# Four modulation units moved from layer 1's attention to layer 2's, shift logits by VectorE's sums, prompt's projection units first in layer 2

## The chip, the cores and the metric

The kernel runs on one core of one Trainium2 chip. The metric is the time on the device in microseconds (us), lower is better. All data are fp32.

## The reference, cut

Two token groups, 128 prompt tokens and 128 sample tokens of width 1024, pass through two layers. Each layer is an attention and a mixture of 16 experts, each with pre-norm, shift, scale and a gated residual. Shift, scale and gate come from six slices of one linear of SiLU(c).

```python
m = jax.nn.silu(cond) @ w_mod[l] + b_mod[l]          # 6 x 1024: shift, scale, gate (attention); shift, scale, gate (experts)
sh, sc, g, shf, scf, gf = jnp.split(m, 6, axis=-1)    # for the prompt's cond and for the sample's
hp, hs = rmsnorm(xp) * (1 + sc_p) + sh_p, rmsnorm(xs) * (1 + sc_s) + sh_s
# layer 1: grouped-query attention and differential attention, layer 2: neighbourhood attention,
# the sample's queries see the sample's keys and 128 cached context keys
xp, xs = xp + g_p * op, xs + g_s * os_
# experts: softmax router, best group of 4, its top 2 experts
h = rmsnorm(x) * (1 + scf) + shf
scores = softmax(h @ w_router)
x = x + gf * sum_e gate_e * ((silu(h @ w_gate[e]) * (h @ w_up[e])) @ w_down[e])
```

The kernel also returns the new keys and values of the prompt. The weights of both layers, some 490 MB, are read from DRAM once.

## The kernel before, in words

**Loads.** SyncE issues all loads of weights, in the order in which its program is written, into a ring of six slots of 2 MB each, of which one unit fills one (`load`, L552 and L554). It waits before each for the unit that had the slot before (`room_for`, `read_at`: a modulation unit signals `mod_used`, another unit signals with its last product). A layer has these dense units: `("in", l, u)`, 512 columns of the input projection, `("out", l, u)`, 512 columns of the output projection, and `("mod", l, group, k)`, a quarter k of the rows of 2048 columns of the modulation's weights. Group 0 is shift and scale of the attention, group 1 the gate of the attention and the shift of the experts, group 2 scale and gate of the experts. `dense_units(l)` gives the order of the dense loads, with the last ones of layer 1 being those of groups of layer 2. `released(l)` gives the order in which their slots come free.

**Experts.** The 16 experts are run in 8 pairs of 12 units. Before a layer's experts begin, some of the first pairs' units are loaded early: `load_ahead`, `load_kept` (quarters of a unit, into buffers that the attention leaves), and `load_first(k)`, into the ring's slots as the attention releases them. In layer 1 all `load_first` stand behind the others (`free = 2 * l` is 0), in layer 2 the first two, the experts' first gate units, are issued ahead of them. Behind these each load waits for the product that used its slot: `load_early` for the rest of pairs 0 to 2, then a loop. The first gate products of the experts are line 1162.

**Order on TensorE and the others.** The attention is cut in 8 turns, four of the sample, then four of the prompt. In a turn scores (L973) are made two turns ahead, ScalarE makes the exponents from them (L1426), VectorE maxima (L1730), reciprocal and shares (L1739, L1750), TensorE transposes the shares (L857), ScalarE copies them (L1437, L1380), TensorE multiplies by the values (L1005, L1011, L1019). What TensorE does beside it stands in a table, `FILL[l]`: items at "front", "head", "keys", "scores" (ahead of the turns), at `(j,)` (in turn j, between transposes and values) and at j (behind the values). In an item's name the second number is the unit and the third the token group (1 sample, 0 prompt). The items: `("in", u, t)` is a projection unit, 8 products of 512 columns (L925); `("mod", l, group, k)` 8 products with `cond` (`mod`, L881) into `sums_bank`; `("modT", g)` and `("nextT", g)` the transposes of a finished group's sums (`mod_transposed`, L892), of this layer or the next; `("wo", u, t)` the output projection (L935); `("rc",)` the shift logits; `hT`, `hk`, `rt`, `xT`, `pos` norm, router and positions of the experts' tokens. VectorE walks the same table (`meanwhile`). On VectorE `mod` copies and adds up a group's result (`modc`, `gates`), and `out_project` (L1782, L1784) multiplies an output by the gate, held in `gbuf`, and adds it to x.

**Gates.** GpSimd writes the attention gates of a layer to DRAM (`spread_gates`, L787), and reads them back to all partitions (L793), into `gbuf`. In layer 2 it waits with the second until VectorE has added the expert outputs and TensorE is done with the sample's scores. `gates_taken` counts the groups whose gates VectorE has put away; SyncE waits for it before its last `load_kept`, too.

**Shift logits.** The router's product is made of normed rows without shift. What the shift adds is a row of 16 numbers, shift times `w_router`, which `shift_logits(l)` makes by 8 products of 128 x 16 (L1051). Layer 1's stands at `("rc",)`, turn 7. Layer 2's stands between the last two scatters of layer 1's experts, in `sums_bank`, and the copy to `rc` of VectorE signals `shift_taken`.

**Modulation of layer 2 in layer 1.** Groups 0 and 1 of layer 2 are read in layer 1: group 0 in turns 2 and 3 with its transposes in turn 4, group 1 at the turns 6 and 7 with its transposes at the end.

## Time and profile before

| | us |
|---|---|
| median of 3 runs | 1247.43 |
| the runs | 1246.78, 1247.43, 1249.86 |
| the profiled execution | 1245.62 |
| its span | 1243.7 |
| first product of layer 1's experts | 194.27 |
| first projection of layer 2 | 641.00 |
| first product of layer 2's experts | 803.78 |

The span is the time from the first to the last instruction in the trace of the profiled execution, whose own time on the device is 1.9 us longer. TensorE is busy for 1163.5 us of the span (94%), VectorE for 279.9, ScalarE for 187.3, GpSimd for 56.4. The granted clock is 0.989 of full speed over the span. The 494.15 MB of the DMA engines are moved at 397 GB/s in the mean, 420 to 431 GB/s while experts run and 182 to 335 GB/s in layer 2's attention. A time in the text is in us from the span's start. The profile counts two instructions for each product, so that a projection unit or a modulation unit, 8 products each, is x16.

### The profile page before, as it was taken

How to read it: one execution, taken by the hardware profiler on the slowest of the kernel's cores; microseconds unless marked ns; L12 is line 12 of the kernel's file. 1: busy time of each engine (PE TensorE's matmuls, PEld its weight loads, DVE VectorE, ACT ScalarE, POOL GpSimd, SP SyncE). 2: the span in 40 equal slices, each digit the busy share in tenths (PEclk: the TensorE clock that was granted, in tenths of full speed). 3: DMA queues.
4: the chain of work that ended last, by engine and by line, in shares of the span. 5: the costliest groups of instructions: out<-in, count | busy, mean ns of one | idle time of the engine just before them, and what ended most of it. 6: DMA issues, size and time to landing. Idle time of an engine off the chain costs nothing.

```text
span 1243.7 us, 13724 instructions
## 1 busy us (share of the span) xinstructions
PE 1163.5 (94%) x5507; PEld 509.5 (41%) x5507; DVE 279.9 (23%) x675; ACT 187.3 (15%) x439; POOL 56.4 (5%) x68
## 2 busy tenths in 40 slices
PE   4999999999988889989999999999999988989898
PEld 2445454443423233434344454653434423343433
DVE  1146533121010101021232354312021110102013
ACT  1224322010000000001021343210000100000010
POOL 0412000000000000000013020000000000000000
PEclk9999999999999999999999999999999999999999
DMA  9999999999999999999995578999999999999997
GB/s 376 386 373 380 414 420 429 421 431 428 428 427 428 428 428 429 429 427 428 418 392 182 196 262 335 391 374 418 428 428 428 427 427 428 428 429 428 428 423 310
DMA packets 63397, 494.15 MB, mean 397 GB/s; under 512 B 5859, under 2 KB 7027, under 8 KB 32117
## 3 DMA queue, kind: packets, MB, share of 16 engines
q1 hardware_dynamic: 60304, 485.85, 94.3%
q0 software_dynamic: 2864, 7.46, 1.9%
q8 instruction: 33, 0.54, 0.2%
q10 hardware_dynamic: 180, 0.17, 0.0%
q14 instruction: 16, 0.12, 0.0%
HBM read 490.69 MB, written 3.16 MB: 397 GB/s over the span
## 4 chain that ended last, share of the span: by engine, by line
PE 71%; DMA 22%; issue 4%; ACT 1%; SPq 1%; DVE 1%; POOL 0%; DVEq 0%; POOLq 0%
PE bank L1162 40%; PE bank L925 12%; DMA ring<-in_w_up 7%; DMA ring<-in_w_gate 7%; DMA ring<-in_w_down 6%; PE bank L935 3%; PE bank L1117 3%; PE bank L1126 3%; PE bank L881 3%; DMA ring<-in_w_in_ab 2%; PE bank L857 2%; PE bank L1188 1%; PE bank L973 1%; PE bank L1218 1%; PE bank L1019 0%
## 5 line engine op out<-in xcount | busy, mean ns | idle before, releaser
L1162 PE MATMUL bank<-ring,hT 128*64 128x512 f32 x2520 | 572.7, 604 | 50.6 <-issue 19.3
L1162 PEld LDWEIGHTS bank<-ring,hT 128*64 128x64 f32 x2520 | 191.2, 139 | 402.6 <-issue 393.6
L925 PE MATMUL bank<-ring,hT 128*128 128x512 f32 x320 | 141.9, 601 | 3.1 <-DMA ring<-in_w_in_ab 2.4
L925 PEld LDWEIGHTS bank<-ring,hT 128*128 128x128 f32 x320 | 60.4, 192 | 80.0 <-issue 77.4
L1940 DVE TENSOR_TENSOR work<-work,bank 128x512 f32<-128x512 f32 x56 | 38.5, 688 | 165.1 <-PE bank L1126 164.9
L1933 DVE TENSOR_TENSOR work<-work,bank 128x512 f32<-128x512 f32 x32 | 22.0, 688 | 222.0 <-PE bank L1162 197.9
L1162 PE MATMUL bank<-work,hT 128*64 128x512 f32 x284 | 69.6, 593 | 0.0
L1117 PE MATMUL bank<-work 128*128 128x128 f32 x512 | 60.4, 276 | 0.0
L1117 PEld LDWEIGHTS bank<-work 128*128 128x128 f32 x512 | 58.7, 192 | 1.7 <-issue 1.6
L1485 ACT ACTIVATE hT<-bank 128x512 f32<-128x512 f32 x32 | 19.0, 595 | 255.3 <-PE bank L1218 255.3
L935 PE MATMUL bank<-ring,work 128*128 128x512 f32 x128 | 56.5, 594 | 0.3 <-DVE work L1759 0.3
L1981 DVE COPY work<-bank 128x512 f32<-128x512 f32 x14 | 9.7, 692 | 207.1 <-PE bank L1162 207.1
L1126 PE MATMUL bank<-work 128*128 128x512 f32 x112 | 51.8, 605 | 0.0
L881 PE MATMUL bank<-ring,cond 128*32 128x512 f32 x384 | 47.0, 614 | 2.1 <-DMA ring<-in_w_mod 1.7
L1188 PE MATMUL bank<-ring,hT 128*64 128x512 f32 x192 | 42.9, 595 | 3.9 <-DMA ring<-in_w_down 3.9
L1921 DVE TENSOR_TENSOR work<-work,bank 128x512 f32<-128x512 f32 x32 | 22.0, 688 | 106.9 <-ACT work L1494 106.9
L1162 PEld LDWEIGHTS bank<-work,hT 128*64 128x64 f32 x284 | 22.7, 137 | 42.1 <-issue 40.7
L1512 ACT ACTIVATE work<-bank 128x512 f32<-128x512 f32 x14 | 8.4, 597 | 191.0 <-PE bank L1162 191.0
L1494 ACT ACTIVATE work<-bank 128x512 f32<-128x512 f32 x32 | 19.1, 597 | 108.5 <-PE bank L1162 108.5
L935 PEld LDWEIGHTS bank<-ring,work 128*128 128x128 f32 x128 | 23.7, 190 | 27.6 <-issue 27.6
L1126 PEld LDWEIGHTS bank<-work 128*128 128x128 f32 x112 | 20.1, 189 | 31.4 <-issue 31.4
L1656 DVE TENSOR_REDUCE hss<-bank 128x8 f32<-128x512 f32 (+1 forms) x16 | 10.5, 658 | 90.2 <-ACT bank L1385 90.2
(214 smaller groups left out, 731.2 us busy)
## 6 DMA issues: line engine op xcount, KB each, us to landing
ring<-in_w_gate SPq DMA_DIRECT2D x56, 2048.0 KB, 17.6
ring<-in_w_up SPq DMA_DIRECT2D x50, 2048.0 KB, 17.2
ring<-in_w_down SPq DMA_DIRECT2D x46, 2048.0 KB, 17.2
ring<-in_w_mod SPq DMA_DIRECT2D x23, 2048.0 KB, 11.8
work<-in_w_up SPq DMA_DIRECT2D x8, 2048.0 KB, 16.1
ring<-in_w_down SPq DMA_DIRECT2D x14, 1024.0 KB, 14.6
ring<-in_w_in_c SPq DMA_DIRECT2D x6, 2048.0 KB, 21.2
ring<-in_w_in_ab SPq DMA_DIRECT2D x4, 2048.0 KB, 21.5
```

Source lines behind the costliest of these rows:

```text
L857: ins = pe.transpose(b[:, i * P:(i + 1) * P], src, K("ident"))
L881: ins = pe.matmul(out, cond[:, 2 * k + r, :], cols, start=(k, r) == (0, 0), stop=(k, r) == (3, 1), tile_position=(0, 32 * j))
L925: ins = pe.matmul(b[:, 0:n], hT[:, c, t * P:(t + 1) * P], w[:, c, 0:n], start=i == 0, stop=i == DC - 1)
L935: ins = pe.matmul(b[:, :], oT(l, t, c), w[:, c, :], start=c == 0, stop=c == DC - 1)
L1117: ins = pe.matmul(bank[2 if first and h else h][:, c * P:(c + 1) * P], htok(t)[:, at:at + P], pick[:, t, :], start=t == 0, stop=t == 1)
L1126: pe.matmul(bank[4 + 2 * t + h][:, :], GT[:, t, :], yd[:, h * UC:(h + 1) * UC], start=True, stop=True).then_inc(m["scattered"], 1)
L1162: ins = pe.matmul(bank[banks[j]][64 * e:64 * e + 64, :], lhs[:, 4 * h + c, 64 * e:64 * e + 64], weights(e, c, j), start=(h, c) == (0, 0), ...
L1188: ins = pe.matmul(bank[banks[j]][64 * e:64 * e + 64, :], lhs[:, 4 * h + c, 64 * e:64 * e + 64], rows4[slots[e]][:, c, j * UC:(j + 1) * UC] ...
L1494: act.activation(sg[:, h * UC:(h + 1) * UC], bank[h][:, :], ACT.Sigmoid).then_inc(m["sig_done"], 1)
L1921: dve.tensor_tensor(hid[:, half], sg[:, half], bank[h][:, :], ALU.mult).then_inc(m["gate_taken"], 1)
L1933: dve.tensor_tensor(hid[:, half], hid[:, half], bank[2 + h][:, :], ALU.mult).then_inc(m["hid_done"], 1)
L1940: dve.tensor_tensor(y[:, t, cols], y[:, t, cols], bank[4 + 2 * t + h][:, :], ALU.add).then_inc(m["y_added"], 1)
```

## The change

1. The four units of `("mod", 1, 1, k)` are no longer loaded and used in layer 1. They are loaded in layer 2 behind its projection units and used at "scores" and in turn 0 there, their transposes stand in turn 1.
2. Layer 1's places: one unit of `("mod", 1, 0, k)` in each of turns 2 and 3, the other two in turn 7, where those of group 1 stood; `("nextT", 0)` stands at the end. SyncE loads two of these units ahead of the output projection's, two behind.
3. In layer 2 the prompt's projection units 0 to 3 stand at "head" and "keys", and the sample's units 4 and 5 (its values) at "scores", between modulation units.
4. `shift_logits`: VectorE multiplies `w_router` by the shift (128 x 128 numbers) and sums over the 8 chunks (`shares_of_shift`, 128 x 16), and one product with the table of ones sums over partitions. It stands in turn 1 of layer 1 and turn 2 of layer 2; the product behind layer 1's experts and its semaphores are gone.
5. In layer 2 SyncE issues three `load_first` ahead of the others in place of two, in layer 1 two in place of none (`free`), and its waits for `gates_taken` and a group's transposes follow the new order.

```diff
     0: {"front": [("in", 0, 1), ("hT", 0, 0), ("in", 1, 1), ("in", 2, 1), ("in", 3, 1)],
...
-        2: [("modT", 2), ("mod", 1, 0, 0), ("mod", 1, 0, 1)],
+        2: [("modT", 2), ("mod", 1, 0, 0)],
...
     if l == 0:
-        return mods(0, 0) + inputs + mods(0, 1) + mods(0, 2) + mods(1, 0) + out + mods(1, 1)
+        later = mods(1, 0)
+        return mods(0, 0) + inputs + mods(0, 1) + mods(0, 2) + later[0:2] + out + later[2:4]
     scales = mods(1, 2)
-    return inputs + scales[0:2] + out + scales[2:4]
+    return inputs + mods(1, 1) + scales[0:2] + out + scales[2:4]
...
-                free = 2 * l
+                free = 2 + l
...
-                sp.wait_ge(gates_taken, 3 + l)
-                sp.wait_ge(filled, fill(("modT", 1, 1 + l)))
+                sp.wait_ge(gates_taken, 2 + 2 * l)
+                sp.wait_ge(filled, fill(("modT", 1, 2 * l)))
...
             def shift_logits(l):
 
-                pe.wait_ge(*emptied_by(("modT", l, 1)))
-                pe.wait_ge(ld_router, 32)
-                b = bank_free(("rc", 0)) if l == 0 else sums_bank
-                for c in range(DC):
-                    ins = pe.matmul(b[:, 0:NE], modc[:, l, 2, 0, c:c + 1].to_broadcast([P, P]), wr[:, c, :], start=c == 0, stop=c == DC - 1)
-                ins.then_inc(filled if l == 0 else shift_ready, 1)
+                pe.wait_ge(ld_const, 16)
+                pe.wait_ge(shift_summed, l + 1)
+                b = bank_free(("rc", l))
+                pe.matmul(b[:, 0:NE], K("ones"), shares_of_shift[:, :], start=True, stop=True).then_inc(filled, 1)
...
-                        if (l, t) == (0, 1):
-                            shift_logits(1)
...
                 modulate(l, 1, 0)
                 if l == 0:
-                    mod(1, 1)
+                    mod(1, 0)
...
+                if group == 1:
+                    dve.wait_ge(*emptied_by(name))
+                    dve.wait_ge(ld_router, 32)
+                    part = cmp[:, 0:128].rearrange("p (c e) -> p c e", c=DC)
+                    then(dve.tensor_tensor(part, wr[:, :, :], modc[:, l, 2, 0, :].unsqueeze(2).to_broadcast([P, DC, NE]), ALU.mult))
+                    dve.tensor_reduce(shares_of_shift[:, :], part.rearrange("p c e -> p e c"), AX.X, ALU.add).then_inc(shift_summed, 1)
...
-                if l == 0:
-                    name = ("rc", 0)
-                    dve.wait_ge(filled, fill(name))
-                    dve.tensor_copy(rc[:, :], bank_of(name)[:, 0:NE]).then_inc(emptied["dve"], 1)
...
+                    elif item[0] == "rc":
+                        name = ("rc", l)
+                        dve.wait_ge(filled, fill(name))
+                        dve.tensor_copy(rc[:, :], bank_of(name)[:, 0:NE]).then_inc(emptied["dve"], 1)
```

What stands in a row on the engines, in the order of their programs, follows for three places. Line numbers of the changed kernel are 2 or 3 lower than those of the kernel before.

TensorE in layer 1 from the end of turn 1 to turn 3, before: x8 of L881 are one modulation unit, L857 transposes, L973 scores, L1011 values, L892 the transposes of a modulation group.

```order
L892 MATMUL bank<-const,m 128x128 x4
L881 MATMUL bank<-ring,cond 32x512 x16
L857 MATMUL bank<-const,work 128x128 x8
L973 MATMUL bank<-work 128x128 x4
L1011 MATMUL bank<-work 64x256 x4
L881 MATMUL bank<-ring,cond 32x512 x8
L857 MATMUL bank<-const,work 128x128 x4
L881 MATMUL bank<-ring,cond 32x512 x8
L857 MATMUL bank<-const,work 128x128 x2
```

The same place, of the changed kernel:

```order
L890 MATMUL bank<-const,m 128x128 x4
L879 MATMUL bank<-ring,cond 32x512 x8
L857 MATMUL bank<-const,work 128x128 x8
L971 MATMUL bank<-work 128x128 x4
L1009 MATMUL bank<-work 64x256 x4
L879 MATMUL bank<-ring,cond 32x512 x8
L857 MATMUL bank<-const,work 128x128 x6
```

Each of the two turns has one modulation unit in place of two.

TensorE in layer 2 from the transposes of the sample's queries and keys to turn 0, before: L925 products are projection units (x8 is one), L1019 values.

```order
L857 MATMUL bank<-const,work 128x128 x24
L925 MATMUL bank<-ring,hT 128x512 x16
L973 MATMUL bank<-work 128x256 x8
L925 MATMUL bank<-ring,hT 128x512 x16
L857 MATMUL bank<-const,work 128x128 x8
L973 MATMUL bank<-work 128x256 x4
L1019 MATMUL bank<-work 64x128 x8
L925 MATMUL bank<-ring,hT 128x512 x8
```

The same place, of the changed kernel:

```order
L857 MATMUL bank<-const,work 128x128 x24
L923 MATMUL bank<-ring,hT 128x512 x16
L971 MATMUL bank<-work 128x256 x8
L879 MATMUL bank<-ring,cond 32x512 x8
L923 MATMUL bank<-ring,hT 128x512 x8
L879 MATMUL bank<-ring,cond 32x512 x8
L923 MATMUL bank<-ring,hT 128x512 x8
L857 MATMUL bank<-const,work 128x128 x8
L971 MATMUL bank<-work 128x256 x4
L1017 MATMUL bank<-work 64x128 x8
L879 MATMUL bank<-ring,cond 32x512 x8
L923 MATMUL bank<-ring,hT 128x512 x8
L879 MATMUL bank<-ring,cond 32x512 x8
```

At "scores" four modulation and projection units stand in turn (each x8), where two projection units stood, and turn 0 has two modulation units more. The projection units of the sample's values stand behind those of the prompt.

SyncE at the end of layer 1's dense loads and the start of the experts' early loads, before: L552 is a modulation unit, L554 an output unit, L564 a unit of an expert.

```order
L552 DMA ring<-in_w_mod 128x2x2048 [waits bank_filled]
L552 DMA ring<-in_w_mod 128x2x2048 [waits mod_used]
L554 DMA ring<-in_w_out_ab 128x8x512 [waits mod_used] x2
L552 DMA ring<-in_w_mod 128x2x2048 [waits mod_used] x4
L564 DMA work<-in_w_up 128x4096 [waits bank_filled]
```

The same place, of the changed kernel:

```order
L554 DMA ring<-in_w_out_ab 128x8x512 [waits bank_filled]
L554 DMA ring<-in_w_out_ab 128x8x512 [waits mod_used]
L552 DMA ring<-in_w_mod 128x2x2048 [waits mod_used] x2
L564 DMA ring<-in_w_gate 128x4096 [waits mod_used] x2
L564 DMA work<-in_w_up 128x4096 [waits bank_filled]
```

The last two of the four modulation units behind the output projection are gone. The experts' first two gate units stand there, ahead of the first `load_ahead`.

## Rows read from the trace of the kernel before

**Rows 1.** windows: us, busy time of PE, PEld, DVE, ACT, POOL, clock, share, GB/s

```profile
200.00:400.00 200.00, 190.76 (x938) 79.42 (x936) 29.36 (x64) 18.99 (x33) 0.00 (x0) 1.00 1.01 427
...
675.00:690.00 15.00, 15.00 (x54) 8.08 (x53) 8.14 (x6) 3.04 (x6) 2.31 (x1) 1.00 0.00 0
803.00:808.00 5.00, 4.22 (x20) 1.61 (x20) 0.00 (x0) 0.60 (x1) 0.00 (x0) 1.00 0.69 268
640.00:800.00 160.00, 157.43 (x697) 84.31 (x696) 62.97 (x164) 52.02 (x143) 22.69 (x20) 1.00 0.76 281
```

**Rows 2.** chain of waits, pairs 1 and 2: start us, us, what

```profile
254.26 20.75 PE bank L1162 x96
...
304.35 20.75 PE bank L1162 x96
```

**Rows 3.** page, part 6: a modulation unit: KB, us to landing

```profile
ring<-in_w_mod SPq DMA_DIRECT2D x23, 2048.0 KB, 11.8
```

**Rows 4.** timeline of SyncE's issues, layer 1, then layer 2

```profile
194.22 0.33 SPq L647 DMA_DIRECT2D m<-in_w_down  x1
201.35 0.80 SPq L564 DMA_DIRECT2D ring<-in_w_down  x2
211.20 0.81 SPq L564 DMA_DIRECT2D ring<-in_w_gate  x2
...
745.10 0.55 SPq L635 DMA_DIRECT2D ring<-in_w_down  x1
759.66 0.33 SPq L564 DMA_DIRECT2D work<-in_w_up  x1
```

**Rows 5.** line views: the issue of 194.22, then those of 201.35

```profile
DMA to landing us min/median/max: 15.1/15.1/15.1
...
DMA to landing us min/median/max: 12.8/15.1/17.4
```

**Rows 6.** line view: a modulation unit issued at 692.83 into an idle queue

```profile
DMA to landing us min/median/max: 7.1/7.1/7.1
```

**Rows 7.** chain of waits, layer 1: start us, us, what

```profile
145.59 0.47 PE bank L892 x4
...
154.87 1.85 PE bank L881 x16
...
178.19 1.69 PE bank L1051 x16
...
194.27 7.09 PE bank L1162 x32
```

**Rows 8.** timeline, layer 1: start us, us, engine, line, what, idle before

```profile
128.74 0.29 DVE L1599 TENSOR_TENSOR cmp<-wr,modc 128x128 f32<-128x128 f32 x1
...
154.90 0.60 ACT L1437 ACTIVATE work<-bank 128x512 f32<-128x512 f32 x1 [4.01 <-PE bank L857]
...
179.02 0.69 DVE L1784 TENSOR_TENSOR x<-x,tmp 128x512 f32<-128x512 f32 x1
```

**Rows 9.** chain of waits, then timeline, layer 2

```profile
641.00 7.11 PE bank L925 x16
...
718.02 1.09 PE L1019 MATMUL bank<-work 128*64 128x128 f32 x16 [0.56 <-ACT work L1437]
```

**Rows 10.** L793 in layer 2, then in layer 1; L787 in layer 2

```profile
DMA to landing us min/median/max: 4.4/4.8/5.1
...
DMA to landing us min/median/max: 8.7/10.3/11.9
...
DMA to landing us min/median/max: 12.2/12.6/13.1
```

**Rows 11.** timeline, layer 2, turns 5 and 6

```profile
762.46 0.88 DVE L1750 TENSOR_SCALAR work<-work,rinv 128x128 f32<-128x128 f32 x4
...
767.29 0.60 PE L857 MATMUL bank<-const,work 128*128 128x128 f32 x4
```

More of the change, by code:

```diff
@@ L113 @@
         0: [("in", 4, 0), ("modT", 1)],
-        1: [("T", 0), ("mod", 0, 2, 2), ("mod", 0, 2, 3)],
-        2: [("modT", 2), ("mod", 1, 0, 0), ("mod", 1, 0, 1)],
-        3: [("mod", 1, 0, 2), ("oT", 1), ("mod", 1, 0, 3)],
-        4: [("wo", 0, 1), ("nextT", 0)],
+        1: [("T", 0), ("rc",), ("mod", 0, 2, 2), ("mod", 0, 2, 3)],
+        2: [("modT", 2), ("mod", 1, 0, 0)],
[2 rows of a table added]
         5: [("wo", 1, 1)],
-        (6,): [("mod", 1, 1, 0)],
         6: [("oT", 0)],
-        (7,): [("mod", 1, 1, 1)],
[2 rows of a table removed]
[2 rows of a table added]
     1: {"front": [("in", 0, 1), ("hT", 0, 0), ("in", 1, 1), ("in", 2, 1), ("in", 3, 1)],
[5 rows of a table removed]
-        2: [("mod", 1, 2, 1)],
[2 rows of a table added]
+        "scores": [("mod", 1, 1, 0), ("in", 4, 1), ("mod", 1, 1, 1), ("in", 5, 1)],
+        0: [("mod", 1, 1, 2), ("in", 4, 0), ("mod", 1, 1, 3)],
+        1: [("T", 0), ("modT", 1), ("mod", 1, 2, 0), ("in", 5, 0)],
+        2: [("rc",), ("mod", 1, 2, 1)],
         3: [("mod", 1, 2, 2)],
@@ L286, in build @@
         rc = sb("rc", [P, NE])
+        shares_of_shift = sb("shares_of_shift", [P, NE])
         lg = sb("lg", [P, NE])
@@ L400, in build @@
         half_squares = sem("half_squares")
-        shift_ready, shift_taken = sem("shift_logits_ready"), sem("shift_logits_taken")
+        shift_summed = sem("shift_summed")
         chunk_ready = {"act": sem("chunk_modulated_act"), "dve": sem("chunk_modulated_dve")}
@@ L865, in mod @@
                     pe.wait_ge(mod_emptied, 3 * l + group)
-                if (l, group, k) == (1, 2, 0):
-                    pe.wait_ge(shift_taken, 1)
                 for r in range(2):
@@ L1219, in hidden_transposed @@
                     ins.then_inc(m["ht_done"], 1)
-                last = number["modT", 1, 1] if l == 0 else number["count", 1]
+                last = number["modT", 1, 0] if l == 0 else number["count", 1]
                 before, behind = ([jobs[k][0] for k in range(last - 6, last + 1) if (bank_of(jobs[k][0]) is bank[1]) == first] for first in (True, False))
@@ L1642, in largest_logit @@
                 if t == 0:
-                    dve.wait_ge(*(emptied_by(("rc", 0)) if l == 0 else (shift_taken, 1)))
+                    dve.wait_ge(*emptied_by(("rc", l)))
                     dve.scalar_tensor_tensor(out=lg[:, :], in0=bank_of(name)[:, 0:NE], scalar=ss[:, 0:1], in1=rc[:, :],
@@ L1990, in experts @@
                 if l == 0:
-                    mod(1, 1)
+                    mod(1, 0)
                 pair(0)
@@ L2009, in experts @@
                     add_last(end, 0, 1)
-                    dve.wait_ge(shift_ready, 1)
-                    dve.tensor_copy(rc[:, :], sums_bank[:, 0:NE]).then_inc(shift_taken, 1)
                     norm_asked(1, 0, 0)
```

13 rows, old and new, of the table FILL are left out of this document.

## The prediction

> **What bounds the kernel now.** Read the table by stretches first. In 200 to 400 us the 16 DMA engines are busy all the time (share 1.01) at 427 GB/s; from 675 to 690 us their share is 0.00 while TensorE is busy 15.00 of 15.00 us; over 640 to 800 us TensorE is busy 157.43 of 160 us, at 281 GB/s [rows 1]. So there are two regimes. While the experts of a layer run, a pair of experts needs 12 units of 2048 KB [rows 3], 25.17 MB, which at 427 GB/s is 58.9 us. The chain of waits shows the same piece in pair 1 (254.26) and in pair 2 (304.35), so TensorE does a pair in 50.1 us [rows 2]. TensorE starts with a store of early loads and uses it up; after that the stream of loads sets the time. In layer 2's attention it is the other way round: TensorE sets the time and the DMA idles. The end of each layer's experts is therefore "when the stream last ran dry, plus bytes over rate", and it runs dry where SyncE has no free buffer to load into.
>
> **Part 1, the loads leave layer 1.** Four units of 2048 KB [rows 3] are 8.39 MB, at 427 GB/s 19.6 us. Layer 1's experts would end 19.6 us earlier if the stream never ran dry. It does. SyncE's last load before the experts' first product is issued at 194.22 [rows 4] and lands 15.1 us later [rows 5], at 209.3. The next, at 201.35, waits until that product gives a buffer back. So at 201.35 there are 209.3 - 201.35 = 7.9 us of work queued. If TensorE reaches the experts X earlier, and 19.6 us of loads are gone, the queue is dry for 19.6 - X - 7.9 us. X can't be over 4 x 1.85 + 0.47 + 1.69 = 9.6 us, all TensorE work that goes (below), so it is dry in any case, and the gain of the stream is not 19.6 but X + 7.9, less what starting a dry queue costs. A load into an empty queue landed 7.1 us after its issue [rows 6]; 2048 KB at 427 GB/s take 4.9; so 2.2 us. At the next issue (211.20, where the second load of 201.35 still had to land, 201.7 + 17.4 = 219.1 [rows 4, 5]) 7.9 us of work become 7.9 - 5.7 = 2.2, just that latency; I take 0.3 us off. Gain of layer 1: X + 5.4.
>
> **X, TensorE's gain in layer 1**, along the chain [rows 7]:
> - Turns 2 and 3 lose a unit each: 3.7 us. But VectorE now makes the shift sums in turn 1, a product of 128 columns (0.29 [rows 8]) and a sum over as many, 0.6 to 0.7 us ahead of its maxima of the next turn, and TensorE's values of turn 2 wait for ScalarE's copy behind those: 0.7 us back. The one-column product, and the values of turn 4, which now meet ScalarE's copy, take 0.5. Left 2.5.
> - The transposes of a modulation group (0.47 at 145.59) go to the end of the attention, where those of the next group stood: 0.4. Sum 2.9.
> - The units of turns 6 and 7 stood where TensorE waits for ScalarE's copy. The unit goes from 154.87 to 156.72, the copy from 154.90 to 155.5 [rows 7, 8], and the values need the copy: of 1.85 us 1.1 is gained, the rest becomes a wait. In turn 7 the transposes need VectorE's shares, made behind the output addition of turn 5, which is itself only 4 us earlier: 0.5 more. Sum 4.5.
> - The eight products of the shift logits (178.19, 1.69, so to 179.88) go, but the transposes behind them need VectorE's addition to x, which ends at 179.02 + 0.69 = 179.71 [rows 7, 8]. Gain 0; the wait takes their place.
>
> So X = 4.5, between 2.9 (nothing in turns 6 and 7) and 9.6 (all of it). Layer 1's experts end 4.5 + 5.4 = **9.9 us** earlier; bounds 8.3 and 15.0. They stay bound by the stream: TensorE has 58.9 - 50.1 = 8.8 us a pair in hand.
>
> The second set of shift products, between the last two scatters of layer 1, stands beside VectorE's and GpSimd's norm of the sample rows, which the next projection needs and they don't: 0 us.
>
> **Part 2, the units come into layer 2.** TensorE is busy there, so they are paid. A unit costs 1.85 us [rows 7], four 7.4. The transposes of the group take 0.5 to 0.7; the one-column product and VectorE's copy, 0.2. The first values of layer 2 waited 0.56 us for ScalarE [rows 9], which had a prompt unit's squares to make first; now value units stand there, which it doesn't touch: -0.5. The loads cost nothing: the first goes out when the layer's fifth projection unit is done, on the old clock at 641.0 + 5 x 7.11 = 676.6 [rows 9], lands 7.1 us later in an idle stretch [rows 1, 6], and is used three units, 21 us, after its issue. The value units of the sample rows come late, but only the first values need them.
>
> One wait grows: that for the gates. GpSimd writes them to DRAM and spreads them back after the last prompt unit, as now. Before, that spreading took 4.4 to 5.1 us with SyncE's queue nearly empty (no issue from 745.10 to 759.66); the same two transfers took 8.7 to 11.9 in layer 1 beside a full queue [rows 4, 10]. Now two more units are queued at that time: the last one of group 2, which waits for the last prompt unit, and the experts' third gate unit, brought forward. So I take 8.7, the first half lands 4.3 us later. VectorE's output addition waits for it, then come shares and maxima. The shares ended at 762.46 + 0.88 = 763.34 and TensorE asked for them at 767.29, 3.95 us later [rows 11]. Of 4.3 us 0.35 come through there, and about 1 more through the last turn's exponents on ScalarE: 1.3 us.
>
> Sum for the start of layer 2's experts: 7.4 + 0.7 + 0.2 - 0.5 + 1.3 = **+9.1 us**. Bounds: 5.7 (the gates not later, and all idle of the stretch, 160 - 157.4 = 2.6, filled) and 14.7 (the gates as in C below). The experts of layer 2 then run as before, only later: in 803 to 808 us the DMA share is 0.69 [rows 1], all early loads had landed when they began, so a third gate load that lands sooner is worth nothing, and the stream starts anew with TensorE.
>
> **Sum.** 9.1 - 9.9 = -0.8 us. Against the profile's own time: span 1243.7 to 1242.9, run 1245.62 to 1244.8. The median of the runs, 1247.43, lies 1.8 us above the profiled run; forecast 1246.6, no change that can be told (about 0.3%, 3.7 us, is what a measurement can tell).
>
> **Two rules of the Trainium skill.** The page "DMA: Bandwidth & Descriptors", section "Queues, rings and completion order", says that each DMA engine takes turns between the queues that have work for it, packet by packet. By it the gates' transfers share with SyncE's units and don't stand behind them, which speaks for 8.7 and against C; layer 1's 8.7 to 11.9 us agree. Its section "Where 436 GB/s comes from" gives about 358 GB/s as the limit of one core's reads from memory; four units would then be 23.4 us. The trace has 427 GB/s, and the measurement decides.
>
> **Rivals.**
> - **A, all of TensorE's gain comes through.** X = 9.6. For: some waits are chains that start at an output projection that is itself earlier. Against: copy and addition end late whatever TensorE does [rows 8]. Then 9.1 - 15.0 = -5.9: 1241.5. Chance 0.16.
> - **B, the stream doesn't run dry.** 9.1 - 19.6 = -10.5: 1236.9. For: no load of layer 1's experts finds the queue empty now. Against: the sum of part 1, dry for any X below 11.7. Chance 0.06.
> - **C, slower: the gates come late.** If their write and spreading stand behind the two added units, 2 x 4.9 = 9.8 us, TensorE waits 9.8 - 3.95 = 5.9 us and the 1 behind it: 6.9 in place of 1.3, so -0.8 + 5.6 = +4.8: 1252.2. It costs from the point where the first half lands 3.95 us later than now, and makes over 0.3% from 8.7 us. For: the write of 4 KB took 12.2 to 13.1 us there already [rows 10]. Against: layer 1's rows. Chance 0.21.
> - That the change doesn't do what it says is excluded by the order of instructions: the units are gone from one place and stand in the other.
>
> **How the numbers follow.** Forecast 0.55, A 0.16, B 0.06, C 0.21; 0.02 for a slower cause that I don't see. The forecast's own terms spread it by about 3.5 us each way, which puts 0.03 of it beyond 3.7 us on the fast side; on the slow side C is that tail. Faster by over 0.3%: 0.16 + 0.06 + 0.03 = 0.25. Slower: 0.21 + 0.02 = 0.23. Within: 0.52. The range takes in A and C and leaves out B and the tails, 1241.0 to 1252.3.
>
> **What the profile after would show.** Right: DMA share well below 1 for 5 to 8 us between 191 and 199 us; the first expert product at about 189.8 instead of 194.27 [rows 7]; layer 2's first projection at about 631 instead of 641.0 [rows 9]; from there to layer 2's first expert product 9.1 us more than before; idle before the transposes of x where the shift products stood. Wrong: expert start in layer 1 near 185 (A); DMA share 1.0 from 100 to 600 us and layer 2's first projection at 621 (B); VectorE waiting 15 us or more for the spread gates, with TensorE idle before the transposes of turn 6 (C).

## The result, and the profile after

The changed kernel runs at **1253.28 us** (median of 6, 1252.37 to 1256.86) against 1247.11 us (median of 6) of the kernel before: ratio 1.0059, 95% interval 1.0048 to 1.0071. Slower by 6.2 us, by more than 0.3%. The forecast was no change, 1246.6 us with a range up to 1252.3. The profiled execution took 1252.37 us against 1245.62.

The page of the changed kernel, the span and two lines of part 2 (40 equal slices of 31.3 us: the DMA engines' busy tenths, and GB/s):

```profile
span 1250.6 us, 13674 instructions
...
DMA  9998979999999999999997789899999999999997
GB/s 375 393 371 347 385 292 377 425 430 427 428 427 427 428 428 429 431 427 428 417 385 242 269 315 396 333 368 412 422 427 428 427 429 429 429 428 429 428 422 297
```

The DMA line of the kernel before reads 9 up to the 21st slice; here the fourth (94 to 125 us) reads 8 and the sixth (156 to 188 us) 7, with 292 GB/s.

The chain of waits of the changed kernel (start us, us, what): the first product of layer 1's experts, one in the stretch in which TensorE waits for loads, layer 2's first projection, and the first product of layer 2's experts.

```profile
193.82 7.09 PE bank L1158 x32
...
362.37 7.09 PE bank L1158 x32
...
637.48 7.10 PE bank L923 x16
...
809.32 7.09 PE bank L1158 x32
```

The rows of the kernel before that answer to the second and the last (the first and the third are in [rows 7, 9]):

```profile
367.23 7.09 PE bank L1162 x32
...
803.78 7.26 PE bank L1162 x32
```

So the time went like this:

| stretch | forecast | measured |
|---|---|---|
| first expert product of layer 1 (194.27 before) | 4.5 earlier | 0.45 earlier |
| what the stream of loads gives beyond that, at the product of 367.23 us before (now 362.37, 4.86 earlier) | 5.4 | 4.4 |
| the same, at layer 2's first projection (641.00 to 637.48, 3.52 earlier) | 5.4 | 3.1 |
| from there to layer 2's first expert product (162.78 to 171.84) | 9.1 longer | 9.06 longer |
| the rest of the span (439.9 to 441.3) | 0 | 1.4 longer |
| span | 0.8 shorter | 6.9 longer |

The rows overlap: the second and the third tell of the same gain at two places, and the span is -3.5 + 9.1 + 1.4. Layer 2's attention came out as forecast. Layer 1 gave 3.5 in place of 9.9 us. Where the first line went is in turn 1 of layer 1. The windows of the changed kernel (columns as in [rows 1]):

```profile
120.00:130.00 10.00, 7.58 (x53) 3.23 (x55) 5.93 (x17) 4.17 (x12) 3.21 (x5) 0.83 0.50 186
...
170.00:180.00 10.00, 8.42 (x30) 4.25 (x29) 1.71 (x4) 2.63 (x8) 0.00 (x0) 1.00 0.53 216
200.00:205.00 5.00, 4.44 (x31) 2.65 (x28) 1.63 (x8) 2.05 (x3) 0.00 (x0) 1.00 0.73 233
```

The same windows of the kernel before:

```profile
120.00:130.00 10.00, 9.81 (x87) 4.28 (x80) 8.39 (x27) 5.72 (x21) 2.61 (x4) 1.00 0.93 338
...
170.00:180.00 10.00, 10.00 (x46) 6.17 (x46) 2.03 (x6) 2.20 (x7) 0.00 (x0) 1.00 1.04 433
200.00:205.00 5.00, 4.44 (x31) 2.65 (x29) 1.41 (x8) 1.61 (x3) 0.00 (x0) 1.00 0.98 402
```

From 120 to 130 us TensorE is busy 7.58 us in place of 9.81, its granted clock is 0.83, and the DMA share is 0.50. The timeline of TensorE there, then the chain's piece behind it (two modulation units), then SyncE's next issue:

```profile
122.24 0.36 PE L1048 MATMUL bank<-shares_of_shift,const 128*128 128x16 f32 x2 [3.40 <-ACT work L1420]
```

```profile
122.60 5.31 PE bank L879 x32
```

```profile
125.52 2.78 SPq L552 DMA_DIRECT2D ring<-in_w_mod  x2
```

The one-column shift product (L1048) waits 3.40 us, and what releases it is ScalarE's exponents (L1420), not VectorE's sums. It writes into a PSUM bank, and the banks go round seven places in the order in which the program asks for them (`bank_free` waits for the one that had the bank seven places before). Seven places before stand the first scores of turn 3, which TensorE has just made, and ScalarE reads them only after VectorE's maxima. VectorE's sums themselves had been ready since 118.3 us. The two modulation units, which need no new bank and so covered that time before the change, stand behind the product. After the idle 3.40 us the clock falls: the two units take 5.31 us, where the kernel before took 3.61 for the same two. They also give up their ring slots late: SyncE's next load goes out at 125.52; before, the corresponding one went out at 120.92. In the kernel before, the two units in the chain, and SyncE's issue:

```profile
119.00 3.61 PE bank L881 x32
```

```profile
120.92 2.08 SPq L554 DMA_DIRECT2D ring<-in_w_out_ab  x2
```

The windows show a second thing, which isn't the product's doing. From 170 to 180 us the DMA share is 0.53 in place of 1.04. SyncE's issues around it, changed and before:

```profile
168.31 0.33 SPq L564 DMA_DIRECT2D ring<-in_w_gate  x1
177.79 0.80 SPq L647 DMA_DIRECT2D work<-in_w_down  x2
```

```profile
162.61 6.46 SPq L564 DMA_DIRECT2D ring<-in_w_gate  x3
...
178.22 0.80 SPq L647 DMA_DIRECT2D work<-in_w_down  x2
```

The issue near 178 us comes at nearly the same time in both. Before it, the kernel before had three units of 2048 KB to queue; the changed kernel had issued two of these at 133 us already and had one left, and the queue ran empty (share 0.19 from 175 to 180 us). So the stream runs dry twice, there and at 195 to 205 us (0.88, then 0.73). The forecast had one dry stretch, 191 to 199 us; from 190 to 195 us the share is 1.01.

### The profile page after: what moved, and what is told of

Read it like the earlier page. It is cut to its first block, busy times and chain, and to the rows that moved or that the text cites. A ratio compares the mean times of both kernels' runs of the same rounds, so it can differ in the third digit from the quotient of the medians.

```text
span 1250.6 us, 13674 instructions
## 1 busy us (share of the span) xinstructions
PE 1163.3 (93%) x5479; PEld 507.0 (41%) x5479; DVE 281.1 (22%) x679; ACT 187.3 (15%) x439; POOL 56.3 (5%) x68
## 4 chain that ended last, share of the span: by engine, by line
PE 67%; DMA 25%; issue 4%; DVE 2%; ACT 1%; SPq 1%; POOL 0%; DVEq 0%; POOLq 0%
PE bank L1158 38%; PE bank L923 12%; DMA ring<-in_w_up 10%; DMA ring<-in_w_down 8%; DMA ring<-in_w_gate 5%; PE bank L933 3%; PE bank L1113 3%; PE bank L879 3%; PE bank L1122 2%; DMA ring<-in_w_in_ab 2%; PE bank L857 1%; PE bank L1184 1%; PE bank L1212 1%; PE bank L971 1%; ACT work L1431 0%
## 5 line engine op out<-in xcount | busy, mean ns | idle before, releaser
L1420 ACT ACTIVATE work<-bank,nm 128x256 f32<-128x256 f32 (+1 forms) x64 | 26.0, 420 | 27.5 <-DVE nm L1728 27.5
```

Source lines behind the costliest of these rows:

```text
L1420: ins = act.activation(PR[:, j % 2, h, 0:nk], bank_of(("S", l, t, b, e))[:, i * nk:(i + 1) * nk], ACT.Exp, bias=nm[:, j % 2, h:h + 1], sca ...
```

## Experiments

The theory after this comparison, **M**: the shift product waits for its bank; TensorE's loss in layer 1 is this wait, with what the clock and the held ring slots add. Against it stood **V**: VectorE's two added operations are late themselves, and hold up scores and exponents wherever the product stands; and **S**: the term for the stream was wrong, that is, loads are worth their bytes or nothing. All ratios are to runs of the kernel before beside them, on the same chip (their medians: 1246.27 us beside runs 1 to 4, 1246.74 beside 5 to 8, 1246.54 beside 9 to 12). They are the ratios on record; the quotient of two medians can differ from them, by 0.0014 at most (run 11).

| run | first expert product | layer 2's first projection | first expert product of layer 2 | median us | ratio (95%) |
|---|---|---|---|---|---|
| before | 194.27 | 641.00 | 803.78 | 1247.11 | |
| changed | 193.82 | 637.48 | 809.32 | 1253.28 | 1.0059 (1.0048 to 1.0071) |
| 1, product behind the units | 189.60 | 633.61 | 805.53 | 1249.73 | 1.0029 (1.0018 to 1.0039) |
| 2, before + shift sums | 202.03 | 647.58 | 810.98 | 1253.88 | 1.0050 (1.0036 to 1.0064) |
| 3, before, 4 loads cut | 195.47 | 639.29 | 802.07 | 1245.02 | 0.9988 (0.9980 to 0.9997) |
| 4, before, 1 load cut | 194.20 | 639.50 | 802.28 | 1244.33 | 0.9984 (0.9975 to 0.9992) |
| 5, as 2, product behind | 194.79 | 639.85 | 803.17 | 1247.80 | 1.0002 (0.9991 to 1.0012) |
| 6, before + layer 2's order | 195.67 | 641.40 | 803.55 | 1246.36 | 0.9993 (0.9984 to 1.0002) |
| 7, changed, 8 products in layer 1 | 188.81 | 632.57 | 804.61 | 1247.64 | 1.0005 (0.9996 to 1.0014) |
| 8, as 7, unit in turn 6 for turn 3 | 189.64 | 632.86 | 803.59 | 1246.45 | 1.0000 (0.9991 to 1.0008) |
| 9, as 7, unit in turn 6 for turn 7 | 188.72 | 632.83 | 803.55 | 1246.27 | 0.9993 (0.9982 to 1.0003) |
| 10, as 7, unit in turn 3 for turn 7 | 191.28 | 634.70 | 805.41 | 1248.35 | 1.0009 (0.9998 to 1.0019) |
| 11, changed, again | 195.00 | 639.36 | 811.24 | 1255.64 | 1.0059 (1.0042 to 1.0076) |
| 12, before, again | 194.65 | 640.82 | 803.59 | 1246.75 | 0.9996 (0.9985 to 1.0007) |

**Run 1: the changed kernel with the shift product behind the two units.**

```diff
-        1: [("T", 0), ("rc",), ("mod", 0, 2, 2), ("mod", 0, 2, 3)],
+        1: [("T", 0), ("mod", 0, 2, 2), ("mod", 0, 2, 3), ("rc",)],
```

> The changed kernel with one item moved: in layer 1's turn 1 the one-column shift product stands behind the two modulation units, not ahead of them. Theory M (the product waits for its PSUM bank, which still holds scores that ScalarE has not read, and the two units that could cover this stand behind it): the 3.6 us wait at 118.6 to 122.2 goes, with it the clock of 0.83 in 120 to 130 us; the first expert product is at 189.5 instead of 193.82, and since the stream of loads hangs on TensorE from 201 us on, the end moves with it: 1249.0 instead of 1253.3. Rival V (VectorE's two added operations are late themselves, wherever the product stands): first expert product at 193 or later, time 1253.

Its window of 120 to 130 us, the first expert product and one in the loads' stretch, from the chain:

```profile
120.00:130.00 10.00, 9.39 (x82) 4.73 (x74) 8.50 (x25) 6.23 (x23) 2.09 (x3) 1.00 0.92 356
```

```profile
189.60 7.09 PE bank L1158 x32
...
359.07 7.09 PE bank L1158 x32
```

The wait is gone, the clock is 1.00, the DMA share 0.92. The first expert product is 4.2 us earlier than in the changed kernel, layer 2's first projection 3.9, the median 3.6 us. M holds; V doesn't explain the loss (what is left of it is in run 5). TensorE now gains 4.67 us in layer 1, where 4.5 were forecast. The stream is still dry at 170 to 175 us (share 0.15), so that hole is the missing loads' and not the wait's.

**Run 2: the kernel before with VectorE's shift sums and the one-column product in place of the eight products, and nothing else**, product at the head of turn 1 of layer 1 and of turn 2 of layer 2 (the edit, cut: the old products and their semaphores go as in the change).

```diff
-        1: [("T", 0), ("mod", 0, 2, 2), ("mod", 0, 2, 3)],
+        1: [("T", 0), ("rc",), ("mod", 0, 2, 2), ("mod", 0, 2, 3)],
...
-        2: [("mod", 1, 2, 1)],
+        2: [("rc",), ("mod", 1, 2, 1)],
...
+                pe.wait_ge(shift_summed, l + 1)
+                b = bank_free(("rc", l))
+                pe.matmul(b[:, 0:NE], K("ones"), shares_of_shift[:, :], start=True, stop=True).then_inc(filled, 1)
```

> The kernel before with the shift logits by VectorE's sums and nothing else changed (product at the head of layer 1's turn 1 and of layer 2's turn 2; all four units stay in layer 1). Theory (the wait is a loss of TensorE only, and costs at the end only where the stream of loads hangs on TensorE): first expert product of layer 1 3.5 to 5 us later than 194.27, near 198.5, but 7.9 us of loads are still queued there, so layer 2's first projection stays at 641 within 1 us; time 1247.5, same as before. Rival (the shift logits cost the whole loss of the change, in any surroundings): 1252 to 1253.

Its window of 120 to 130 us, the product's wait, SyncE's next issue:

```profile
120.00:130.00 10.00, 6.59 (x38) 1.90 (x35) 7.08 (x19) 3.96 (x14) 4.25 (x7) 0.66 0.27 89
```

```profile
123.74 0.58 PE L1049 MATMUL bank<-shares_of_shift,const 128*128 128x16 f32 x2 [3.41 <-ACT work L1421]
```

```profile
127.95 2.81 SPq L555 DMA_DIRECT2D ring<-in_w_out_ab  x2
```

I was wrong here: I expected the queue to take up the loss. The same wait, 3.41 us, a clock of 0.66, and the two output units, issued at 120.92 before, go out at 127.95, 7.0 us later, with a DMA share of 0.27. (This trace was 1.3 us behind that of the kernel before already ahead of the wait, see run 5.) In this kernel all units are in layer 1 and the stream isn't dry later (no window of 5 us from 130 to 225 us has a share under 0.97), and so a hole in it counts in full: from 110 to 135 us the DMA engines moved 2.6 MB less than before, 6.1 us at 427 GB/s, and layer 2's first projection is 6.6 us later. The 7.9 us that are queued at 201 us cover a late TensorE, but not a late issue at 121 us. The shift logits, which I had priced at 1.2 us in layer 1 (0.7 for the sums, 0.5 for the product and the values of turn 4), cost nearly as much by themselves as the whole change: 1.0050 against 1.0059.

**Runs 3 and 4: the kernel before with four, or one, of the group's loads cut to an eighth.** TensorE's work stays; part of the modulation is left out.

```diff
+                    if (l, group) == (1, 1) and k in (0, 1, 2, 3):
+                        sp.dma_start(rows2[slot][:, :, 0:256], src[:, :, 0:256]).then_inc(dense_ld[slot], 16)
+                    else:
+                        sp.dma_start(rows2[slot][:, :, :], src).then_inc(dense_ld[slot], 16)
```

> The kernel before with its four loads of modulation group 1 of layer 2 cut to an eighth (256 of 2048 columns, so these units use what was in the buffer before: part of the modulation is left out); TensorE's work is the same. 17.2 us of loads at 427 GB/s are gone, X is 0. Theory (the stream runs dry at 201 us, where 7.9 us of work are queued): gain at layer 2's first projection 4.3 to 5.4 us (636), time 1242. Rival (the stream doesn't run dry, loads are worth their bytes): gain 17, projection at 624, time 1230.

> The kernel before with one of these four loads cut to an eighth (part of the modulation left out), 4.3 us of loads less. Theory (7.9 us are queued at 201 us, so a first unit is worth its bytes and the later ones next to nothing): gain 4.3 us, projection at 636.7, time 1243, within 1 us of the kernel with four cut. Rival (gain in proportion to bytes, a quarter of what four give): 1 to 1.4 us, time 1246.

The product in the loads' stretch, with four cut, then with one cut and that kernel's last products of layer 1 (chain of waits; 367.23 and 626.86 before):

```profile
364.38 7.09 PE bank L1165 x32
```

```profile
362.87 7.09 PE bank L1165 x32
```

```profile
623.65 8.78 PE bank L1191 x32
```

One cut load gives 4.36 us there, its full bytes (4.3). Four give 2.85, with a first expert product that is 1.2 us later, so 4.05 beyond TensorE. S falls in both readings: the first unit counts in full, the other three count nothing, since from 201 us on the stream hangs on TensorE. But I missed the other place: at layer 2's first projection the gain is 1.71 us with four cut and 1.50 with one, not 4.3 and more, and the medians are 1.3 and 1.9 us below before, not 4. In the kernel with one cut all of what is missing has a row. The last load that the end of layer 1 waits for is issued 4.31 us earlier than before (605.43 to 609.74), but takes 18.09 us to land in place of 16.99, and the last products of layer 1 take 8.78 us in place of 7.09 (granted clock 0.69 from 625 to 630 us, 1.00 before). That load and those products in the kernel before:

```profile
609.74 16.99 DMA ring<-in_w_down
...
626.86 7.09 PE bank L1188 x32
```

**Run 5: run 2 with the product behind the units.**

> The kernel before with the shift logits by VectorE's sums, as in the run that had them ahead of the two modulation units of layer 1's turn 1, but now with the product behind these units. Theory M (the product waits for a PSUM bank that holds scores not yet read; the units behind it are held, they free ring slots late, and the stream of loads, which sets the end of layer 1 when all units are in it, stands still): no idle DMA between 121 and 130 us beyond what the kernel before has, first expert product at 194.3 to 195.3, layer 2's first projection at 641 to 642, time within 1 us of before. Rival V (VectorE's added sums hold up scores and exponents wherever the product stands): first expert product at 198 or later, time 1251 or more.

```profile
120.00:130.00 10.00, 9.40 (x86) 4.27 (x78) 8.43 (x27) 5.53 (x20) 2.55 (x4) 1.00 0.95 332
```

The first expert product is at 194.79, the ratio 1.0002: the loss of run 2 is gone by the place of one instruction. (Projection 639.85, a little earlier than expected.)

VectorE's sums do cost TensorE something, and it shows once a spread of the traces is taken out. The traces differ by up to 1.6 us already at 114 us, ahead of anything that the change touches on TensorE in layer 1. The transposes of a modulation group there, before and in run 5:

```profile
114.36 0.63 PE L892 MATMUL bank<-const,m 128*128 128x128 f32 x4
```

```profile
114.12 0.63 PE L891 MATMUL bank<-const,m 128*128 128x128 f32 x4
```

From these transposes to the first expert product it is 79.90 to 79.91 us in all five traces whose layer 1 is that of the kernel before on TensorE (before, runs 3, 4, 6, 12), and 80.67 us in run 5. So V was right for 0.8 us, where the prediction had 0.7 for the sums; the rest of the loss of run 2 was the place of the product. In this kernel the 0.8 us don't reach the end, which hangs on the loads.

**Run 6: the kernel before with layer 2's order of projection units alone.**

```diff
-        "head": [("in", 4, 1), ("in", 5, 1)],
-        "keys": [("in", 0, 0), ("in", 1, 0)],
-        "scores": [("in", 2, 0), ("in", 3, 0)],
+        "head": [("in", 0, 0), ("in", 1, 0)],
+        "keys": [("in", 2, 0), ("in", 3, 0)],
+        "scores": [("in", 4, 1), ("in", 5, 1)],
```

> The kernel before with only the order of layer 2's projection units changed (the prompt's units 0 to 3 at head and keys, the sample's units 4 and 5 at scores). The prediction's term: the wait of 0.56 us of the first values for ScalarE goes and nothing takes its place, so from layer 2's first projection to its first expert product 162.3 instead of 162.78 us, time 0.5 us lower than before, which is not to be told from no change. Rival (the value units now come so late that the first turn's values or VectorE's scores wait for them): 163.5 or more.

From projection to expert product 162.15 us, 0.63 less: as forecast (0.5), too small to be told in the median. It shows another thing: its first expert product is 1.4 us later than before with the same layer 1, and layer 2's first projection only 0.4. That is how a layer bound by its loads takes a late TensorE. The 1.4 us stand there at 114 us already (transposes at 115.77 in place of 114.36): the first expert product scatters by that much with one and the same program.

**Run 7: the changed kernel with layer 1's shift logits by the eight products in turn 7.**

```diff
-        1: [("T", 0), ("rc",), ("mod", 0, 2, 2), ("mod", 0, 2, 3)],
+        1: [("T", 0), ("mod", 0, 2, 2), ("mod", 0, 2, 3)],
...
-        7: [("hT", 1, 1), ("wo", 0, 0), ("rt", 1), ("hk", 1), ("wo", 1, 0), ("xT",), ("mod", 1, 0, 2),
+        7: [("hT", 1, 1), ("wo", 0, 0), ("rt", 1), ("hk", 1), ("wo", 1, 0), ("rc",), ("xT",), ("mod", 1, 0, 2),
```

> The changed kernel with layer 1's shift logits as in the kernel before: eight products in turn 7, no sums on VectorE in layer 1; layer 2 as changed. Theory M: TensorE's wait of 3.4 us in turn 1 is gone, and with it VectorE's 0.65 us and the one-column product: first expert product at 188.5 to 189.5 (the eight products hide behind VectorE's addition to x), the end follows it: 1248.5 to 1249.5 instead of 1253.3. Rival (the eight products are paid, 1.7 us): first expert product at 190.5 or later.

```profile
188.81 7.09 PE bank L1166 x32
...
357.25 7.09 PE bank L1166 x32
```

The first expert product is at 188.81, so the eight products hide behind VectorE's addition to x, as the prediction had it. The ratio is 1.0005 (median 1247.64, below the 1248.5 to 1249.5 expected): undoing the shift logits of layer 1 gives back nearly all that the change lost. Counted from the transposes at 114 us, the first expert product comes 74.16 us later here, 74.95 in run 1: the 0.8 us of VectorE's sums again.

**Runs 8, 9 and 10: places for the units.** All have the eight products in layer 1 and, in layer 2, the moved group's transposes behind the next modulation unit.

```diff
-        1: [("T", 0), ("modT", 1), ("mod", 1, 2, 0), ("in", 5, 0)],
+        1: [("T", 0), ("mod", 1, 2, 0), ("modT", 1), ("in", 5, 0)],
```

SyncE's order of loads follows where a unit changes its place. Run 8 moves `("mod", 1, 0, 1)` from turn 3 to `(6,)`, run 9 `("mod", 1, 0, 2)` from turn 7 to `(6,)`, run 10 the same unit from turn 7 to turn 3.

> A version made from what the runs showed: layer 1's shift logits by eight products in turn 7, one of layer 2's group 0 units moved from turn 3 into turn 6 of layer 1, where TensorE waits for ScalarE's copy and it costs about 0.75 of its 1.85 us, and in layer 2 the transposes of the moved group behind the next modulation unit (0.67 us of waiting). Theory (from 201 us on the stream hangs on TensorE, so what TensorE gains the end gains): first expert product at 187.5 to 188.5, layer 2's first projection at 631, its first expert product 171.2 us later, time 1246.5, equal to the kernel before within 1 us. Rival (the stream is bound by its own dry places ahead of 190 us, where ring slots are held): first expert product earlier but the first projection of layer 2 no earlier than 633.5, time 1249.

> The changed kernel with layer 1's shift logits by eight products (as in the run of that name), the moved group's transposes of layer 2 behind the next modulation unit, and one of the two units of turn 7 of layer 1 in turn 6. From the two runs before: in turn 6 such a unit costs 0.7 us (outputs at 157.21 instead of 156.40), in turn 7 it is on TensorE's path with 1.85. Theory: first expert product at 187.7 (188.81 less 1.1), layer 2's first projection at 631.5, then 170.7 us to its first expert product, time 1245, 1.5 us below the kernel before. Rival (turn 7's unit is hidden too, and turn 6's is paid): first expert product at 189.5.

> As the kernel with the unit in turn 6, but with this unit in turn 3 as a second one there. The run without any unit in turn 3 had the output projection at 135.51 against 135.41 with one: in turns 2 and 3 TensorE waits for VectorE's maxima. Theory (that wait has room for a second unit in part): output projection at 136 to 137, first expert product at 187.5 to 188.5. Rival (no room left): output projection at 137.3, first expert product at 188.8.

The start of the first output projection with one unit in turn 3 (run 7), none (run 8) and two (run 10), from the chain of waits:

```profile
135.41 6.87 PE bank L933 x16
```

```profile
135.51 6.87 PE bank L934 x16
```

```profile
137.30 6.87 PE bank L933 x16
```

Read as they stand, the one unit of turn 3 is free and the second is paid in full. But the three traces are not equally late at 114 us (transposes at 114.65, 115.39 and 114.73). Counted from there the projection starts after 20.76 us with one unit, 20.12 with none and 22.57 with two: the first unit costs 0.6 of its 1.85 us, the second 1.8. I missed run 8 for that reason: its unit gave up 0.6 us in turn 3 and cost 0.7 in turn 6, and the first expert product stayed where it was (74.25 us from the transposes, 74.16 in run 7). Run 9 missed too: moving the unit of turn 7 to turn 6 gave 0.2 us (73.93), not 1.1. Run 10's rival was nearer (projection as it said), but its first expert product came later still, at 191.28; why, no run shows. The transposes behind the unit took 1.3 us off layer 2: 170.73, 170.72 and 170.72 us in these three, 172.04 in run 7. The best of them, run 9, has 0.9993 (0.9982 to 1.0003): none beats the kernel before by more than the measurement tells.

**Runs 11 and 12: the two kernels once more.**

> The changed kernel once more, for a second trace. The layer 2's experts took 1.3 us longer after it than before it (437.92 to 436.59 us), with no difference in their loads. Theory (it is the spread of executions): in the second traces of the two kernels this difference is another, of either sign, within 1.5 us; what stands ahead of it repeats: 443.66 and 171.84 us. Rival (the change costs the experts of layer 2 a fixed amount): again 1.3.

> The kernel before once more, for a second trace beside that of the changed one on the same chip. Theory: 446.7 us from the first expert product to layer 2's first projection, 162.8 from there to its first expert product, and 436.6 to 438 us for the rest, since 436.59 is the lowest of eight traces. Rival: 436.6 again.

The product in the loads' stretch, changed and before:

```profile
365.48 7.09 PE bank L1158 x32
```

```profile
366.98 7.09 PE bank L1162 x32
```

The ratio repeats, 1.0059. In the second pair the span from the first expert product of layer 2 is 442.1 us changed and 440.7 before (the two expectations count to a point 3.3 us ahead of the span's end), again 1.4 longer, so my theory (spread alone) lost this pair. The stretches ahead of it in run 11 are 444.4 us (443.7 in the first trace) and 171.9 (171.8). Over all traces it is 440.8 to 442.4 (mean 441.7) in the seven with units in layer 2, and 439.9 to 442.2 (mean 440.9) in the seven without. The ranges overlap; whether the change costs layer 2's experts 0.8 to 1.4 us stays open, and no run was made that tells why.

## Why the prediction was wrong

**What bounds the kernel: right, but for a dry place.** Layer 1's experts are bound by a stream that is dry at 201 us once units are taken out (DMA share 0.73 from 200 to 205 us, 0.98 before), layer 2's attention by TensorE. The longer dry place, 165 to 180 us, was not foreseen, and the sign that the prediction named, a share well below 1 between 191 and 199 us, came late and in part: 1.01 from 190 to 195 us, 0.88 from 195 to 200.

**X, the failing step: "The one-column product, and the values of turn 4, which now meet ScalarE's copy, take 0.5."** The product was priced as an instruction, not as a place in the rotation of the banks; its wait for a bank was not in the sum at all. The sum was 2.9 us up to the output projections; the second of these, and the third, in the chain of waits of the changed kernel:

```profile
148.79 6.88 PE bank L933 x16
...
161.41 6.87 PE bank L933 x16
```

and before:

```profile
147.56 6.87 PE bank L935 x16
...
161.84 6.87 PE bank L935 x16
```

At the second projection TensorE is 1.2 us late in place of 2.9 early, 4.1 us off. The wait of 3.40, the product's 0.36 and the 1.70 that the two units lose by the clock (5.31 against 3.61) make 5.5 us, where the sum had 1.2 for all that the shift logits cost ahead of this projection: 4.3 us more than priced, less the 0.2 us by which this trace was ahead at 114 us. Run 1, with the product behind the units, brings X to 4.67. The rest of the step holds: turns 6 and 7 were to give 1.6 and give 1.7 (1.2 late to 0.4 early), and the eight products in turn 7 were hidden (run 7). In the changed kernel the transposes of x wait for VectorE where they stood:

```profile
179.33 0.94 PE L857 MATMUL bank<-const,x 128*128 128x128 f32 x6 [1.58 <-DVE x L1780]
```

**X + 5.4, mis-sized.** The form is right (runs 3 and 4). Against the first trace of before, the part beyond X at 362 us is 4.4 in the changed kernel and 2.5 in its second trace, 3.5 in run 1, 4.0 in run 3, 4.5 in run 7, 2.7 in run 9. At layer 2's first projection it is 3.1 and 2.4, 2.7, 2.9, 3.0, 2.6. I had taken off 2.2 us for one load into an empty queue, and 0.3 for the next issue. The landings of the two loads issued at 200.90 us, and of the two issued at 210.75:

```profile
DMA to landing us min/median/max: 7.7/9.9/12.2
...
DMA to landing us min/median/max: 9.1/11.3/13.6
```

The first pair's later load took 12.2 us in place of 17.4: 5.2 us beyond X, near the 7.9 - 2.2 of the sum. The second pair's took 13.6 in place of 17.3, 3.7 us beyond X: the next issue cost 1.5 us (2.2 in run 1, 1.1 in run 4), not 0.3. The loss between 362 us and the end of the layer has a row as well. The load that the layer's last products wait for:

```profile
604.89 18.31 DMA ring<-in_w_down
```

It is issued 4.85 us earlier than before (609.74), so until then nothing was lost, and takes 1.3 us longer to land (18.31 against 16.99); in run 1 it takes 0.9 us longer, in run 4 1.1. Why it takes longer stays open. With run 1's X the layer gives 7.4 us, not 9.9. So of the 7.7 us between the forecast span (0.8 shorter) and the measured one (6.9 longer) X has 4.1, the stream's term 2.3, and the open rest behind layer 2's attention 1.4.

**Layer 2, +9.1: right to 0.1 us, with terms that cancel.** I had 1.3 us for late gates. VectorE's wait, TensorE's asking for the shares behind it, and the landing of the two spreading transfers, changed kernel:

```profile
767.79 0.69 DVE L1778 TENSOR_TENSOR tmp<-bank,gbuf 128x512 f32<-128x512 f32 x1 [10.38 <-DMA gbuf<-gate_rows]
...
768.52 0.69 DVE L1780 TENSOR_TENSOR x<-x,tmp 128x512 f32<-128x512 f32 x1
...
769.33 0.87 DVE L1746 TENSOR_SCALAR work<-work,rinv 128x128 f32<-128x128 f32 x4
...
772.61 0.60 PE L857 MATMUL bank<-const,work 128*128 128x128 f32 x4
```

```profile
DMA to landing us min/median/max: 7.4/8.0/8.6
```

The first half took 7.4 us (I took 8.7), the addition ends at 768.52 + 0.69, and TensorE asks at 772.61, 2.4 us after the shares are made (769.33 + 0.87): no wait. The Trainium skill, page "DMA: Bandwidth & Descriptors", section "Queues, rings and completion order", has the engines take turns between queues; 7.4 to 8.6 us beside two queued units agree with it. In place of that term stands one that I had not: the transposes of the moved group wait for a bank too.

```profile
735.33 0.72 PE L890 MATMUL bank<-const,m 128*128 128x128 f32 x4 [0.67 <-ACT work L1420]
```

0.67 us. Four units 7.4, transposes 0.72, product 0.4, this wait 0.7, the order -0.6 (run 6) make 8.6; 0.5 us of the 9.06 has no row of its own. Two runs narrow it. Runs 2 and 5 have layer 2's shift logits without the four units and take 163.40 and 163.32 us for this stretch, 162.78 before: 0.5 to 0.6 us for the product with VectorE's sums, not 0.4. And the transposes' place cost 1.3 us (runs 8 to 10), twice the wait that has a row.

**The rivals.** A and B fell: X was below the forecast, and the stream ran dry. C's time (1252.2) is nearest to the result by luck, since its mechanism did not happen: TensorE waits for no gates. A slower outcome by a cause I did not see had 0.02 of my chances; it was what happened. **The range**, 1241.0 to 1252.3, missed the median by 1.0 us; the bank's wait was in none of its ends.

## What to carry to other kernels

A short instruction is as dear as the buffer it asks for: before moving one in a schedule with rotating banks, count back the rotation and see who reads that bank last, and put the work that covers the wait ahead of it. When loads are taken out of a stream that is near its limit, the first unit is worth its bytes at most and the next ones only what the consumer gains: cut one load, then all, compare, and compare at the end of the stage too (here 4.4 us in the middle had become 1.5 at the end). A late release of a load buffer, early in a stream that never runs dry, counts in full, whatever is queued later. And before two traces are compared at a late point, compare them at a point ahead of the change: here they differed by up to 1.6 us there.

## What the runs showed of the hardware

In the three traces with it, TensorE's granted clock fell behind the 3.4 us wait of the shift product. The two units behind it took 5.31 us (changed kernel), 6.15 (run 11) and 6.06 (run 2) in place of 3.6. Over 120 to 130 us the granted clock was 0.83 in the changed kernel and 0.66 in run 2, that is, a part of these 10 us at 1.2 in place of 2.4 GHz. Run 2's two units:

```profile
124.32 6.06 PE bank L880 x32
```

In runs 1, 5 and 7, without the wait, the clock there was 1.00. So this wait cost half to three quarters of its own length on top. The same shows where TensorE waits for loads in the kernel before: behind an idle time of 2.89 us that ends at 406.36 us, the expert products behind it (x32) take 8.78 us in place of 7.09, with a granted clock of 0.68 from 405 to 410 us.
